# Expert layer: a ring of fifteen U blocks until the pick lists are turned, its first four blocks loaded at the end of the query projection

## The chip, the cores and the metric

The kernel runs as one launch on one core of a Trainium2 chip. The time is that of the whole launch in device microseconds (us); lower is better. Five engines work side by side: TensorE (PE, its weight loads PEld), VectorE (DVE), ScalarE (ACT), GpSimd (POOL) and SyncE (SP), which issues most of the transfers. GpSimd issues the indirect ones. Transfers between HBM and the on-chip memory are carried by 16 DMA engines.

## The reference, cut to what matters

The program is a hybrid block (`first_block`), which the change leaves alone, followed by a block of two layers. Each of those is a token mixer, a layer norm, an expert layer with 16,384 experts in which each token takes 16 for each of 8 heads, and another layer norm:

```python
def peer_ffn(h, w_query, sub_keys, expert_u, expert_v):
    q = (xt @ w_query).reshape(T, PEER_HEADS, 2, HALF_Q).astype(jnp.float32)
    scores = jnp.einsum('thpc,hpnc->thpn', q, sub_keys.astype(jnp.float32))
    top_s, top_i = lax.top_k(scores, PEER_TOPK)
    cand_s = top_s[:, :, 0, :, None] + top_s[:, :, 1, None, :]
    cand_i = top_i[:, :, 0, :, None] * N_KEYS + top_i[:, :, 1, None, :]
    ...
    best_s, best_pos = lax.top_k(cand_s, PEER_TOPK)
    idx = jnp.take_along_axis(cand_i, best_pos, axis=-1)
    gate = jax.nn.softmax(best_s, axis=-1)
    ...
    def expert_chunk(args):
        xc, ic, gc = args
        u = expert_u[ic]
        act = jax.nn.gelu(jnp.einsum('cd,ced->ce', xc, u).astype(jnp.float32), approximate=False)
        v = expert_v[ic]
        return jnp.einsum('ce,ced->cd', (gc * act).astype(v.dtype), v)
```

There are 256 tokens of width 1024, all in float32. An expert number is `i * 128 + j`, with one part from each half of the query.

## The kernel before

`second_layer` ends with two stages that matter here. `project` multiplies by `w_query_2`, fed by SyncE with slabs of the weight, while VectorE already chooses the best keys of some heads (`FirstChoice`). Then `small_experts` does the expert layer. It treats the two tiles of 128 tokens differently:

- **The dense tile** is scored against all experts. These are cut into 128 blocks of 128 experts; block n has a U block and a V block of 512 KB each. `dense(n)` on TensorE takes U block n and the turned tokens in 8 matmuls to the scores, `gelu(n)` on ScalarE writes the activation to slot `n % E`, `gate(n)` on VectorE multiplies it by the gates, and `back(n)` multiplies it by V block n in two matmuls of 512 columns.
- **The sparse tile** has for each of its 128 picks one row of 1 MB in all (u and v of each token's own expert, called a pair row), gathered by GpSimd (`load_picks`). `pick(s)` on VectorE takes one product with a running sum (L2688), ScalarE makes the share of it (`share`, L2611 and L2613), and one pick later VectorE adds the scaled v half (L2699).

All instructions stand in a fixed order on each engine, written by loops. In the order of TensorE: the scores of the keys; `LISTS_AFTER` (41) dense blocks; the turning of the pick lists (`turn_lists`, L2514), for which VectorE must have chosen the picks of the dense tile (`select(1)`, ending at L2805); 16 groups of `spread` (L2522), which turn one-hot rows into the gate matrix G, with dense blocks between them up to block E (68); `sum_gates`; then `back(0)` to `back(127)` with the other N − E blocks spread evenly over the first `DENSE_SPAN` (104) of them. VectorE slips the first 15 picks into `select(1)` and one into each of the 16 groups; the others lie beside the backs. ScalarE does the share of pick s after the gelu that `SHARES_AFTER[s]` names, and the exponentials of the gates after those in `EXP_AFTER`.

SyncE issues the U loads in block order. A U block goes to one of `RAW_U` = 4 places and waits until the block that had the place is scored (`load_u`, L2456). V blocks have 7 places; three are loaded at U blocks 5 to 7, four when G is made; from V block 10 on GpSimd gathers only those rows that some token chose (L2660). Pair rows have a ring of 4. Each ring place has a semaphore of its own.

The memory: `all_gates` (128 KB of each partition) holds G in its first half; before G exists, that half holds the query columns, the keys and what the selection works on. The upper part holds the four U places, the pair ring and the turned tokens. An arena of 68 KB holds the activation slots, the V places and, over the last four V places, the one-hot buffers.

Of the kernel before, what the change touches and what calls it, by code (L numbers as in the profile page):

```python
# [23 lines left out]
P = 128  # L24
# [170 lines left out]
def project(nc, S, name, rows, weights, slabs, cols=None, norm_scale=None, evacuate=None, scaled=None, loads=(),  # L195
            raw=None, banks=tuple(range(BANKS)), ring=2, act_from=None, beside=None, norm=None,
            ahead=None, above=0, tops_early=False, extra=None, late_loads=(), also=None, busy=(0, 0, 0, 0), loads_last=False, heads=None):
# [28 lines left out]
    with phase(nc, "slab_in0 slab_in1 slab_in2 unit_done squares mean_sq rstd_root rstd_done rows_scaled "  # L226
# [2117 lines left out]
EARLY = 68  # L2344
RAW_U, RAW_V = 4, 7
RING = 4
# [6 lines left out]
def small_experts(nc, S, layer, spare, norm):  # L2353
# [3 lines left out]
    N, E, PICKS = NKEYS, EARLY, PH * TOPK  # L2357
# [14 lines left out]
    with phase(nc, "dve_step x_turned h_full_done scores_done scores_out exp_ready exp_done rows_done lists_t lists_out "  # L2372
# [3 lines left out]
        phase(nc, "u_in0 u_in1 u_in2 u_in3 v_in0 v_in1 v_in2 v_in3 v_in4 v_in5 v_in6 row_in0 row_in1 row_in2 row_in3 "  # L2376
# [3 lines left out]
        u_in, v_in = landed[:RAW_U], landed[RAW_U:RAW_U + RAW_V]  # L2380
        row_in, some_in = landed[RAW_U + RAW_V:RAW_U + RAW_V + RING], landed[RAW_U + RAW_V + RING:]
# [40 lines left out]
        upper = S["upper"]  # L2422
        raw_u = upper([P, RAW_U, D])
# [13 lines left out]

        def slot(n):
            return act[:, n % E, :]
# [10 lines left out]
        with nc.Block() as block:  # L2450
            @block.sync
            def _(sp):
                def load_u(n):
                    if n >= RAW_U:
                        sp.wait_ge(scored, n - RAW_U + 1)
                    sp.dma_start(raw_u[:, n % RAW_U, :], ud(n)).then_inc(u_in[n % RAW_U], 16)  # L2456

                def load_v(n):
                    if n >= RAW_V:
                        sp.wait_ge(y_done, n - RAW_V + 1)  # L2460
                    sp.dma_start(raw_v[:, n % RAW_V, :], vd(n)).then_inc(v_in[n % RAW_V], 16)

                for n in range(E):
                    load_u(n)
                    if 5 <= n < 8:
                        load_v(n - 5)
                for n in range(E, E + RAW_U):
                    load_u(n)
                sp.wait_ge(g_done, SPREAD)
                for n in range(3, RAW_V):  # L2470
                    load_v(n)
                for n in range(N):
                    if n + RAW_V < WHOLE:
                        load_v(n + RAW_V)
                    for m in dense_after(n):
                        if m + RAW_U < N:
                            load_u(m + RAW_U)
                    if n == DENSE_SPAN:
                        sp.wait_ge(scored, N)
                        sp.dma_start(raw_u[:, 0, :], one_row(S, "ln2_g_2", layer)).then_inc(ln_in, 16)  # L2480
                        sp.dma_start(raw_u[:, 1, :], one_row(S, "ln2_b_2", layer)).then_inc(ln_in, 16)

            @block.tensor
            def _(pe):
# [16 lines left out]
                def dense(n):  # L2501
                    bank = (4 if n < E else 0) + n % 2
                    pe.wait_ge(u_in[n % RAW_U], 16 * (n // RAW_U + 1))
                    if n >= 2:
                        pe.wait_ge(acted, n - 1)
                    for c in range(KD):
                        last = nc.tensor.matmul(PS[:, bank, 0:P], raw_u[:, n % RAW_U, c * P:(c + 1) * P], h_full[:, c, :],  # L2507
                                                start=(c == 0), stop=(c == KD - 1), skip_group_check=True)
                    last.then_inc(scored, 1)
# [535 lines left out]
def second_layer(nc, S, layer, base, norm_of):  # L3045
    dram = S["dram"]
    if True:
# [57 lines left out]
        with ExitStack() as peer:  # L3105
# [14 lines left out]
            S["idx"] = spare([P, 2 * PH, TOPK]).bitcast(U32)  # L3120
            with phase(nc, "head_scored head_copied head_chosen") as (_, head_scored, head_copied, head_chosen):
# [73 lines left out]
```

## Time and profile before

| | us |
|---|---|
| median of 3 runs | 2655.43 |
| lowest and highest of them | 2653.43, 2655.89 |
| the profiled execution | 2652.92 |
| its span | 2651.1 |

Shares of the span: TensorE 87%, VectorE 57%, ScalarE 24%, GpSimd 23%; mean DMA rate 300 GB/s. The two expert layers reach from about 1147 to 1794 and from about 2000 to the end of the span. A busy TensorE is not one at its peak, and in rings of buffers an engine that waits for a transfer may be at the end of a chain of such waits. So the page's totals are read only to find the stages, and each stage is then read by its own windows, waits and order of time. 1.8 us of the profiled execution lie outside its span.

### The profile page before, as it was taken

The page shows a single profiled execution, that of the slowest core. Times are in us where ns is not written, and L with a number is a line of the kernel's source. Part 1 is how long each engine was busy: PE and PEld are TensorE (multiplying, and loading weights), DVE is VectorE, ACT ScalarE, POOL GpSimd, SP SyncE. Part 2 cuts the span into 40 slices and gives each one's busy share as a digit, 9 for nine tenths or more (in the row PEclk, how much of TensorE's full clock was granted, in tenths as well). Part 3 has the DMA queues.
Part 4 walks back from the last instruction along what each step waited for, and adds up shares of the span by engine and source line. Part 5 has one row for each costly group of instructions (what it writes and reads, how often), then busy time and mean ns, then how long its engine had stood idle before and what let it go on. Part 6 is the DMA issues. An engine that isn't in the chain of part 4 may idle for free. (4 is left out here: it accounts for less than half of the span.)

```text
span 2651.1 us, 42435 instructions
## 1 busy us (share of the span) xinstructions
PE 2312.0 (87%) x16666; PEld 1696.5 (64%) x16668; DVE 1514.8 (57%) x2992; ACT 627.9 (24%) x1546; POOL 599.8 (23%) x637
## 2 busy tenths in 40 slices
PE   8988988999998779987898888878998699888885
PEld 8987875555544377787875555528788597554542
DVE  4787552211100045589976566675468996666666
ACT  4543322100000036322321111114532232111111
POOL 0011200111111000001224454540000223454453
PEclk9999989999999989999899999999999999999999
DMA  7420025999999863369999999987237989999997
GB/s 224 152 73 3 3 112 213 407 418 419 419 419 420 362 220 128 105 226 385 350 398 411 408 406 412 403 338 247 76 120 268 397 341 408 407 405 403 405 402 280
DMA packets 223238, 794.92 MB, mean 300 GB/s; under 512 B 37909, under 2 KB 103957, under 8 KB 165312
## 3 DMA queue, kind: packets, MB, share of 16 engines
q1 hardware_dynamic: 148496, 443.86, 43.4%
q0 software_dynamic: 74544, 348.34, 33.2%
q8 instruction: 134, 2.20, 0.3%
q14 instruction: 64, 0.52, 0.1%
HBM read 881.07 MB, written 11.27 MB: 337 GB/s over the span
## 5 line engine op out<-in xcount | busy, mean ns | idle before, releaser
L2540 PE MATMUL psum<-v_raw,act 128*128 128x512 f32 x1024 | 500.4, 621 | 144.0 <-DMA v_raw<-expert_v_dram,all_gates 143.7
L2507 PEld LDWEIGHTS psum<-all_gates 128*128 128x128 f32 x4096 | 501.2, 198 | 115.9 <-issue 64.8
L2507 PE MATMUL psum<-all_gates 128*128 128x128 f32 x4096 | 512.0, 282 | 44.1 <-DMA all_gates<-expert_u_dram 41.0
L2652 POOL DMA_INDIRECT all_gates<-expert_pairs_dram,all_gates x256 | 260.8, 1019 | 1117.4 <-DVE all_gates L2795 500.0
L2540 PEld LDWEIGHTS psum<-v_raw,act 128*128 128x128 f32 x1024 | 182.0, 193 | 371.2 <-DMA v_raw<-expert_v_dram,all_gates 220.9
L2688 DVE CUSTOM_DVE_ANT_0 all_gates<-all_gates,psum 128x1024 f32<-128x1024 f32 x194 | 236.8, 1221 | 305.5 <-DMA all_gates<-expert_pairs_dram,all_gates 303.5
L2699 DVE SCALAR_TENSOR_TENSOR psum<-all_gates,psum 128x1024 f32<-128x1024 f32 x254 | 326.1, 1284 | 1.0 <-ACT all_gates L2613 0.7
L1754 PE MATMUL psum<-piece_raw,tile_cols 128*64 128x256 f32 x2496 | 287.9, 381 | 17.8 <-DMA piece_raw<-w_up_dram 7.7
L1754 PEld LDWEIGHTS psum<-piece_raw,tile_cols 128*64 128x64 f32 x2496 | 176.7, 137 | 129.3 <-issue 35.5
L2660 POOL DMA_INDIRECT v_raw<-expert_v_dram,all_gates x236 | 234.1, 992 | 77.8 <-issue 70.8
L2611 ACT ACTIVATE all_gates<-all_gates 128x1 f32<-128x1 f32 x256 | 51.6, 201 | 753.6 <-DVE all_gates L2688 753.6
L1834 DVE TENSOR_TENSOR hidden<-silu,psum 128x256 f32<-128x256 f32 x39 | 16.4, 421 | 276.4 <-PE psum L1754 276.4
L454 PE MATMUL psum<-in_cols,in_top 128*128 128x256 f32 x864 | 160.2, 287 | 8.9 <-DVE in_low L362 3.9
L1789 PE MATMUL psum<-piece_raw,hidden_cols 128*64 128x512 f32 x624 | 143.2, 595 | 10.5 <-DMA piece_raw<-w_down_dram 10.1
L454 PEld LDWEIGHTS psum<-in_cols,in_top 128*128 128x128 f32 x864 | 135.3, 193 | 11.9 <-issue 7.3
L346 DVE TENSOR_TENSOR in_low<-in_raw,in_top 128x2048 fp32r<-128x2048 f32 x38 | 87.0, 2290 | 68.1 <-ACT in_top L297 68.1
L454 PE MATMUL psum<-in_cols,in_low 128*128 128x256 f32 x432 | 122.8, 284 | 0.0
L2592 ACT ACTIVATE act<-psum 128x128 f32<-128x128 f32 x256 | 67.9, 268 | 217.2 <-PE psum L2507 216.8
L1812 ACT ACTIVATE silu<-psum 128x256 f32<-128x256 f32 x39 | 15.0, 385 | 415.9 <-PE psum L1754 415.9
L1840 DVE COPY tile_result<-psum 128x512 f32<-128x512 f32 x39 | 27.0, 691 | 130.4 <-PE psum L1789 130.4
L1789 PEld LDWEIGHTS psum<-piece_raw,hidden_cols 128*64 128x64 f32 x624 | 43.8, 137 | 88.2 <-issue 70.0
L2832 DVE TENSOR_TENSOR act<-act,all_gates 128x128 f32<-128x128 f32 x256 | 90.4, 374 | 6.5 <-ACT all_gates L2596 6.5
(541 smaller groups left out, 3392.4 us busy)
## 6 DMA issues: line engine op xcount, KB each, us to landing
all_gates<-expert_u_dram SPq DMA_DIRECT2D x256, 512.0 KB, 7.7
piece_raw<-w_gate_dram SPq DMA_DIRECT2D x78, 1024.0 KB, 19.5
piece_raw<-w_up_dram SPq DMA_DIRECT2D x78, 1024.0 KB, 21.6
piece_raw<-w_down_dram SPq DMA_DIRECT2D x78, 1024.0 KB, 22.7
in_raw<-w_in_dram SPq DMA_DIRECT2D x48, 1024.0 KB, 5.2
query_raw<-w_query_dram SPq DMA_DIRECT2D x16, 1024.0 KB, 5.5
v_raw<-expert_v_dram SPq DMA_DIRECT2D x20, 512.0 KB, 7.3
w_o<-w_o_dram SPq DMA_DIRECT2D x16, 512.0 KB, 11.1
```

Source lines behind the costliest of these rows:

```text
L346: nc.vector.tensor_tensor(r32(lows[place[s]]), raw[:, s % RING, :, :], tops[place[s]], ALU.subtract).then_inc(slab_low, 1)
L454: last = nc.tensor.matmul(PS[:, banks[n % len(banks)], half * T:(half + 1) * T], r32(lhs), r32(rhs), start=(k == 0 and i == 0), stop=(k == ...
L1754: last = nc.tensor.matmul(PS[side(g), bank, 0:WIDE], window[:, t % 2, k, :], raw[:, n % RAW, at:at + WIDE], start=(k == 0), stop=(k == KD ...
L1789: last = nc.tensor.matmul(PS[side(g), OUT[t % 2], :], hid_cols[:, c, q - 4, :], raw[:, n % RAW, at:at + HALF], start=(q == 4 and c == 0), ...
L2507: last = nc.tensor.matmul(PS[:, bank, 0:P], raw_u[:, n % RAW_U, c * P:(c + 1) * P], h_full[:, c, :], start=(c == 0), stop=(c == KD - 1), s ...
L2540: last = nc.tensor.matmul(PS[:, 4 + m, :], slot(n), raw_v[:, n % RAW_V, m * BANK:(m + 1) * BANK], start=(n == 0), stop=(n == N - 1), skip_ ...
L2592: nc.scalar.activation(slot(n), PS[:, bank, 0:P], ACT.Gelu).then_inc(acted, 1)
L2652: nc.gpsimd.indirect_dma_start(out=ring[:, r, :, :].rearrange("p h d -> p (h d)"), out_offset=None, in_=S["pair_rows"], in_offset=bass.Ind ...
L2660: nc.gpsimd.indirect_dma_start(out=raw_v[:, n % RAW_V, :], out_offset=None, in_=S["v_rows"], in_offset=bass.IndirectOffsetOnAxis(ap=load_r ...
L2688: nc.vector.tensor_tensor_reduce(row, row, own, 1.0, 0.0, ALU.mult, ALU.add, own_sum[:, s:s + 1]).then_inc(dotted, 1)
L2699: stt(both, row, own_share[:, c:c + 1], both, ALU.mult, ALU.add).then_inc(picked_done, 1)
L2832: tt(slot(n), slot(n), G[:, :, n], ALU.mult).then_inc(gated, 1)
```

## The change

Four things are done together:

- The U ring has 15 places until block 45: the four old ones, four over the one-hot buffers of the arena, and seven over the query columns and keys at the start of `all_gates`. From block 45 on it is the ring of 4 again. The first load into the seven waits until all key scores are made. Eleven more semaphores go with it.
- The loads of blocks 0 to 3 stand at the end of SyncE's part of the query projection, through a new argument `behind`. Their four semaphores are made in a phase of their own around the projection and the expert layer.
- E goes from 68 to 80: `EARLY` = 72 slots in the arena, 8 more in `all_gates` behind G. The blocks spread beside the backs are 48 in place of 60.
- `LISTS_AFTER` goes from 41 to 52, `EXP_AFTER` from (8, 38) to (8, 49), and the shares move to later gelus.

```diff
+                if behind is not None:
+                    behind(sp)
                 if loads:
                     sp.wait_ge(loaded, 16 * (len(loads) + len(late_loads)))
...
-EARLY = 68
+EARLY = 72
+MORE = 8
 RAW_U, RAW_V = 4, 7
+OVER_HOTS, OVER_QUERY = 4, 7
+WIDE_U = RAW_U + OVER_HOTS + OVER_QUERY
+WIDE_UNTIL = 3 * WIDE_U
...
-    N, E, PICKS = NKEYS, EARLY, PH * TOPK
+    N, E, PICKS = NKEYS, EARLY + MORE, PH * TOPK
...
-    EXP_AFTER = (8, 38)
-    LISTS_AFTER = 41
+    EXP_AFTER = (8, 49)
+    LISTS_AFTER = 52
...
-    SHARES_AFTER = (19, 20, 21, 23, 24, 26, 28, 29, 30, 32, 34, 35, 36, 38, 39)
+    SHARES_AFTER = (21, 22, 24, 26, 28, 31, 34, 36, 39, 41, 44, 46, 47, 49, 50)
...
+        def u_place(n):
+            return n % WIDE_U if n < WIDE_UNTIL else (n - WIDE_UNTIL) % RAW_U
+
+        def u_before(n):
+            return max((m for m in range(n) if u_place(m) == u_place(n)), default=None)
...
         def slot(n):
-            return act[:, n % E, :]
+            return act[:, n % E, :] if n % E < EARLY else more_act[:, n % E - EARLY, :]
...
                 def load_u(n):
-                    if n >= RAW_U:
-                        sp.wait_ge(scored, n - RAW_U + 1)
-                    sp.dma_start(raw_u[:, n % RAW_U, :], ud(n)).then_inc(u_in[n % RAW_U], 16)
+                    if u_before(n) is not None:
+                        sp.wait_ge(scored, u_before(n) + 1)
+                    if n == RAW_U + OVER_HOTS:
+                        sp.wait_ge(scores_done, len(BATCHES[0]) + len(BATCHES[1]))
+                    sp.dma_start(u_buffer(n), ud(n)).then_inc(u_in[u_place(n)], 16)
...
                 for n in range(E):
-                    load_u(n)
+                    if n >= RAW_U:
+                        load_u(n)
                     if 5 <= n < 8:
                         load_v(n - 5)
...
+            def first_blocks(sp):
+                for n in range(RAW_U):
+                    sp.dma_start(S["raw_u"][:, n, :], S["u_src"](n)).then_inc(first_u_in[n], 16)
```

The queue of SyncE in the first layer, from the last slabs of the query weight into the expert layer. Before (L268 loads slabs, L2456 U blocks, L2461 V blocks):

```order
L268 DMA query_raw_11086<-w_query_dram 128x8x256 x5
L252 UNCONDITIONAL_BRANCH
L2451 UNCONDITIONAL_BRANCH
L2456 DMA all_gates<-expert_u_dram 128x1024 x6
L2461 DMA v_raw_12104<-expert_v_dram 128x1024
...
L2456 DMA all_gates<-expert_u_dram 128x1024 x64
L2461 DMA v_raw_12104<-expert_v_dram 128x1024 x6
```

Now (L3159 is `first_blocks`, L2485 the other U loads, L2490 V blocks):

```order
L268 DMA query_raw_11086<-w_query_dram 128x8x256 x5
L3159 DMA all_gates<-expert_u_dram 128x1024 x4
L252 UNCONDITIONAL_BRANCH
L2478 UNCONDITIONAL_BRANCH
L2485 DMA u_over_hots_12111<-expert_u_dram 128x1024 x2
L2490 DMA v_raw_12109<-expert_v_dram 128x1024
...
L2485 DMA all_gates<-expert_u_dram 128x1024 x11
L2485 DMA u_over_hots_12111<-expert_u_dram 128x1024 x4
L2485 DMA all_gates<-expert_u_dram 128x1024 x11
L2485 DMA u_over_hots_12111<-expert_u_dram 128x1024 x4
L2485 DMA all_gates<-expert_u_dram 128x1024 x46
L2490 DMA v_raw_12109<-expert_v_dram 128x1024 x7
```

Four U loads moved from behind the branch between the two stages to a place ahead of it, and the U loads ahead of the V blocks that wait for G are 84 in place of 72.

TensorE in the first layer, from the first dense block to the second group of the gate matrix; a dense block is 8 matmuls. Before (L2507 dense, L2514 the lists, L2522 a group):

```order
L2507 MATMUL psum<-all_gates 128x128 x328
L2514 MATMUL psum<-constants_51,all_gates 128x128 x4
L2522 MATMUL psum<-hot_j_12108,hot_i_12106 128x128 x8
L2507 MATMUL psum<-all_gates 128x128 x8
L2522 MATMUL psum<-hot_j_12108,hot_i_12106 128x128 x8
```

Now (L2537 dense, L2544 the lists, L2552 a group):

```order
L2537 MATMUL psum<-all_gates 128x128 x32
L2537 MATMUL psum<-all_gates,u_over_hots_12111 128x128 x32
L2537 MATMUL psum<-all_gates 128x128 x88
L2537 MATMUL psum<-all_gates,u_over_hots_12111 128x128 x32
L2537 MATMUL psum<-all_gates 128x128 x88
L2537 MATMUL psum<-all_gates,u_over_hots_12111 128x128 x32
L2537 MATMUL psum<-all_gates 128x128 x112
L2544 MATMUL psum<-constants_51,all_gates 128x128 x4
L2552 MATMUL psum<-hot_j_12115,hot_i_12113 128x128 x8
L2537 MATMUL psum<-all_gates 128x128 x8
```

Ahead of the lists there are 416 dense matmuls (52 blocks) in place of 328 (41 blocks), and the places of their U blocks go round the wide ring.

## Rows read from the trace of the kernel before

**Rows 1.** page, part 2: the span in 40 slices of 66.3 us each
```profile
DMA  7420025999999863369999999987237989999997
GB/s 224 152 73 3 3 112 213 407 418 419 419 419 420 362 220 128 105 226 385 350 398 411 408 406 412 403 338 247 76 120 268 397 341 408 407 405 403 405 402 280
```

**Rows 2.** stages of layer one: window, busy us (x instructions), clock, DMA share, GB/s
```profile
1148.50:1265.70 117.20, 89.82 (x704) 85.43 (x703) 106.84 (x405) 29.26 (x86) 18.50 (x18) 0.93 0.95 361
1271.50:1351.00 79.50, 78.90 (x678) 78.38 (x679) 76.94 (x91) 30.47 (x74) 18.40 (x16) 0.97 0.93 353
1352.00:1722.00 370.00, 317.34 (x1415) 196.25 (x1415) 229.10 (x354) 51.25 (x224) 177.04 (x179) 0.97 1.02 409
1722.00:1782.00 60.00, 40.78 (x83) 15.01 (x82) 43.25 (x64) 9.44 (x35) 33.05 (x34) 0.97 0.97 379
```

**Rows 3.** the same view in windows of ten us, both layers
```profile
1130.00:1140.00 10.00, 10.00 (x87) 10.00 (x85) 8.73 (x30) 2.67 (x3) 0.00 (x0) 1.00 0.01 2
1150.00:1160.00 10.00, 10.00 (x92) 10.00 (x91) 9.83 (x57) 5.50 (x11) 0.00 (x0) 1.00 0.75 266
1160.00:1170.00 10.00, 8.33 (x72) 7.95 (x72) 9.83 (x63) 1.11 (x4) 0.00 (x0) 1.00 1.00 375
...
1270.00:1280.00 10.00, 8.46 (x54) 8.46 (x55) 10.00 (x12) 2.59 (x7) 1.97 (x2) 0.67 0.40 137
2000.00:2010.00 10.00, 9.25 (x83) 9.28 (x84) 8.76 (x54) 5.91 (x10) 0.00 (x0) 1.00 0.63 222
```

**Rows 4.** DMA, 1193 to 1262: queues, then issues with us to landing
```profile
DMA packets 5424, 26.70 MB, mean 387 GB/s; under 512 B 607, under 2 KB 607, under 8 KB 3729
...
q0 software_dynamic: 1902, 13.84, 50.2%
q1 hardware_dynamic: 3516, 12.79, 48.0%
...
all_gates<-expert_u_dram SPq DMA_DIRECT2D x24, 512.0 KB, 9.0
all_gates<-expert_pairs_dram,all_gates POOLq DMA_INDIRECT x13, 9.4
```

**Rows 5.** SyncE queue in order of time: start, us, line, what
```profile
1107.48 18.08 SPq L268 DMA_DIRECT2D query_raw<-w_query_dram  x4
1147.77 2.00 SPq L2456 DMA_DIRECT2D all_gates<-expert_u_dram  x4
```

**Rows 6.** TensorE in order of time, first layer
```profile
1153.67 10.88 PE L2507 MATMUL psum<-all_gates 128*128 128x128 f32 x96
...
1265.75 1.12 PE L2514 MATMUL psum<-constants,all_gates 128*128 128x128 f32 x4 [6.99 <-DVE all_gates L2805]
1271.54 3.78 PE L2522 MATMUL psum<-hot_j,hot_i 128*128 128x128 f32 x16 [4.67 <-DVE hot_j L2825]
...
1352.41 7.14 PE L2530 MATMUL psum<-all_gates,ident_half 128*128 128x512 bf16 x31
```

**Rows 7.** VectorE in order of time, first layer
```profile
1192.47 1.22 DVE L2688 CUSTOM_DVE_ANT_0 all_gates<-all_gates,x 128x1024 f32<-128x1024 f32 x1
...
1202.44 1.29 DVE L2696 TENSOR_SCALAR psum<-all_gates 128x1024 f32<-128x1024 f32 x1 [6.05 <-ACT all_gates L2613]
...
1261.79 1.22 DVE L2688 CUSTOM_DVE_ANT_0 all_gates<-all_gates,x 128x1024 f32<-128x1024 f32 x1 [2.52 <-DMA all_gates<-expert_pairs_dram,all_gates]
...
1265.40 0.29 DVE L2805 TENSOR_TENSOR all_gates<-all_gates 128x128 f32<-128x128 f32 x1
```

**Rows 8.** waits, 1352 to 1782: total us, times, longest
```profile
DVE all_gates L2688 <- DMA all_gates<-expert_pairs_dram,all_gates: 152.8, 93, 3.8
...
PEld psum L2540 <- DMA v_raw<-expert_v_dram,all_gates: 109.2, 63, 4.5
```

**Rows 9.** end of the program in order of time
```profile
2641.94 2.48 DVE L2280 SCALAR_TENSOR_TENSOR x<-x,ln_stats,all_gates 128x1024 f32<-128x1024 f32 x2
2646.25 0.40 SPq L2885 DMA_DIRECT2D out_dram<-x  x1
```

More of the change, by code:

```diff
@@ L196, in project @@
             raw=None, banks=tuple(range(BANKS)), ring=2, act_from=None, beside=None, norm=None,
-            ahead=None, above=0, tops_early=False, extra=None, late_loads=(), also=None, busy=(0, 0, 0, 0), loads_last=False, heads=None):
+            ahead=None, above=0, tops_early=False, extra=None, late_loads=(), also=None, busy=(0, 0, 0, 0), loads_last=False, heads=None, behind=None):
     PS, C = S["psum"], S["const"]
@@ L2350, with small_experts @@
 UPPER_FLOATS = RAW_U * D + RING * 2 * D + KD * P + 7 * PH * TOPK
-def small_experts(nc, S, layer, spare, norm):
+def small_experts(nc, S, layer, spare, norm, first_u_in):
     PS, C = S["psum"], S["const"]
     HP = 2 * PH
-    N, E, PICKS = NKEYS, EARLY, PH * TOPK
+    N, E, PICKS = NKEYS, EARLY + MORE, PH * TOPK
     DENSE, SPARSE = 0, 1
@@ L2379, in small_experts @@
             memory3, ln_in, scored, acted, gated, y_done, picked_done, quarter_done, root_ready, root_done):
-        u_in, v_in = landed[:RAW_U], landed[RAW_U:RAW_U + RAW_V]
-        row_in, some_in = landed[RAW_U + RAW_V:RAW_U + RAW_V + RING], landed[RAW_U + RAW_V + RING:]
+        over = OVER_HOTS + OVER_QUERY
+        u_in, v_in = list(first_u_in) + list(landed[:over]), landed[over:over + RAW_V]
+        row_in, some_in = landed[over + RAW_V:over + RAW_V + 8], landed[over + RAW_V + 8:]
         KB = 1024
@@ L2421, in small_experts @@
         number = spare([P, P])
-        upper = S["upper"]
-        raw_u = upper([P, RAW_U, D])
+        upper, raw_u = S["upper"], S["raw_u"]
         ring = upper([P, RING, 2, D])
@@ L2436, in batch_number, with u_turn, u_buffer @@
             return turn * len(BATCHES[0]) + BATCHES[turn].index(n) + 1
+        u_over_query = S["all_gates"][:, 0:OVER_QUERY * D // NKEYS, :].rearrange("p (b r) j -> p b (r j)", b=OVER_QUERY)
+        def u_place(n):
+            return n % WIDE_U if n < WIDE_UNTIL else (n - WIDE_UNTIL) % RAW_U
+        def u_turn(n):
+            return sum(u_place(m) == u_place(n) for m in range(n + 1))
+        def u_before(n):
+            return max((m for m in range(n) if u_place(m) == u_place(n)), default=None)
+        def u_buffer(n):
+            place = u_place(n)
+            if place < RAW_U:
+                return raw_u[:, place, :]
+            if place < RAW_U + OVER_HOTS:
+                return u_over_hots[:, place - RAW_U, :]
+            return u_over_query[:, place - RAW_U - OVER_HOTS, :]
         def slot(n):
-            return act[:, n % E, :]
+            return act[:, n % E, :] if n % E < EARLY else more_act[:, n % E - EARLY, :]
         def picks_after(n):
@@ L2506, in dense @@
                     for c in range(KD):
[L2507 removed]
+                        last = nc.tensor.matmul(PS[:, bank, 0:P], u_buffer(n)[:, c * P:(c + 1) * P], h_full[:, c, :],
                                                 start=(c == 0), stop=(c == KD - 1), skip_group_check=True)
@@ L3120, in second_layer @@
             S["idx"] = spare([P, 2 * PH, TOPK]).bitcast(U32)
+            u, v = dram["expert_u_2"], dram["expert_v_2"]
+            S["u_src"] = lambda j: u[bass.ds(layer * NKEYS + j, 1), :, :, :].rearrange("j p k i -> (j p) k i")
+            S["v_src"] = lambda j: v[bass.ds(layer * NKEYS + j, 1), :, :].rearrange("j i d -> (j i) d")
+            S["raw_u"] = S["upper"]([P, RAW_U, D])
+            first_u_in = peer.enter_context(phase(nc, "u_in0 u_in1 u_in2 u_in3"))[1:]
+            def first_blocks(sp):
+                for n in range(RAW_U):
+                    sp.dma_start(S["raw_u"][:, n, :], S["u_src"](n)).then_inc(first_u_in[n], 16)
             with phase(nc, "head_scored head_copied head_chosen") as (_, head_scored, head_copied, head_chosen):
@@ L3124, in second_layer @@
                         raw=ahead["raw"], loads=[(S["keys"], one("sub_keys_2", "p e n"))], norm=between, ahead=ahead,
-                        above=3 * 16 * KB, banks=(0, 1, 2, 3, 4, 5),
+                        above=3 * 16 * KB, banks=(0, 1, 2, 3, 4, 5), behind=first_blocks,
                         heads=FirstChoice(nc, S, head_scored, head_copied, head_chosen))
-            u, v = dram["expert_u_2"], dram["expert_v_2"]
-            S["u_src"] = lambda j: u[bass.ds(layer * NKEYS + j, 1), :, :, :].rearrange("j p k i -> (j p) k i")
-            S["v_src"] = lambda j: v[bass.ds(layer * NKEYS + j, 1), :, :].rearrange("j i d -> (j i) d")
             S["pair_rows"] = dram["expert_pairs_2"][:, :]
             S["v_rows"] = v.rearrange("j i d -> (j i) d")
-            small_experts(nc, S, layer, spare, norm_of("ln2_b_2", layer, None) if layer + 1 < LAYERS else None)
+            small_experts(nc, S, layer, spare, norm_of("ln2_b_2", layer, None) if layer + 1 < LAYERS else None, first_u_in)
 def layout(inputs):
```

8 lines of the change are left out of this document (5 added, 3 removed).

## The prediction

> **What bounds the kernel now.** I read the page's 40 slices first [rows 1]. In slices 18 to 26 and 31 to 39, counted from 0, DMA stands near 9 tenths and mostly about 400 GB/s: the expert layers are streams of transfers. The slices also show holes where those layers begin. So I cut the first expert layer into its stages [rows 2]. Stage A reaches from the first U load (1148.5) to the turned lists (1265.7): DMA share 0.95, but only 361 GB/s. Stage B (1271.5 to 1351), the 16 groups: 353 GB/s, while TensorE is busy 78.90 of 79.50 us and VectorE 76.94. Stage C (1352 to 1722), backs with U blocks beside them: share 1.02, 409 GB/s. Stage D (1722 to 1782), backs without U blocks: 379 GB/s.
>
> Stage C is bound by DMA. TensorE is idle 53 of 370 us there and VectorE 141, GpSimd 193, and over C and D the large waits all end with a transfer: VectorE 152.8 us for pair rows, TensorE's weight loads 109.2 us for V rows [rows 8]. No engine's work fills the stage, and the two streams that wait share the same 16 engines with U. So its length follows its bytes: what is loaded before G is made need not be loaded in C.
>
> The ten-us windows show where DMA has room [rows 3]. From 1130 to 1140 it moves 2 GB/s: the last query slab is issued by 1125.6 and the first U load only at 1147.77 [rows 5]. In 1150 to 1160 the share is 0.75 and 266 GB/s. With only U moving and the share at 1.00 (1160 to 1170) it still gives 375 GB/s, and TensorE, waiting for blocks, is busy 8.33 of 10. The second layer starts in the same way (2000 to 2010: 0.63, 222 GB/s).
>
> What ends stage A is VectorE: the lists were turned at 1265.75 after a wait of 6.99 for L2805, which starts at 1265.40 [rows 6, 7]. VectorE has two pauses on its way: 6.05 us before 1202.44, when ScalarE's first share stands behind the gelu of block 19, which TensorE gets late, and 2.52 us for a pair row before 1261.79.
>
> **The change part by part, per layer.** A U block is 512 KB, 0.524 MB.
>
> 1. Stage C loses blocks. E goes from 68 to 80, so 12 fewer blocks, 12 × 0.524 = 6.29 MB. At C's own 409 GB/s that is **15.4 us less**. TensorE also loses 12 × 1.8 = 22 us of work there (1.8 us a block: six blocks in 10.88 [rows 6]), so it gets no closer to being the bound. Bounds of the term: 15.4 if the rate stays, 16.6 at D's 379, 0 if the stage did not follow its bytes.
>
> 2. Stage A must load more before the lists. Before: 361 GB/s × 117.2 us = 42.3 MB; of it 41 + 4 U blocks (23.6 MB) and 3 V blocks (1.6), which leaves 17.1 MB of pair rows. Now 52 blocks must be there, but four came early: 48 × 0.524 = 25.2, with V and the same pair rows 43.9 MB. The only question is the rate. At 409 that takes 107.3 us, at 387 (the mean of 1193 to 1262 [rows 4]) 113.4, at the 375 of U alone 117.1. With 1.8 us for the last block the lists could be turned at 1257.6, 1263.7 or 1267.4. VectorE sets the other limit: without its 6.05 us pause L2805 starts at 1259.4. That pause should go: share 0 now stands behind block 21, and 22 blocks are scored by 1153.7 + 22 × 1.8 = 1193.3 if they have landed; by then DMA at 375 has moved 16.8 MB, less V and about 3 MB of pair rows, 23 blocks and the early four. I take the middle rate: lists at about 1263.7, **2 us earlier**, with bounds of 6 earlier and 2 later from these rates.
>
> The early four transfers are issued behind the last slab and take 2.1 / 0.409 = 5 us in a stretch where DMA moves 2 GB/s; nothing is queued behind them but the stage's end, and TensorE is still full with the projection in 1130 to 1140. I charge nothing for them; were they in the way, it would be by at most those 5 us. The load of block 8 now waits for the last key score; behind it on SyncE stand only further U loads, and the four blocks and three V blocks ahead of it (3.7 MB, 9 us at 409) cover from 1148.5 to 1157, past the first dense block at 1153.67, which follows those scores.
>
> 3. Stage B gets one block more (28 instead of 27), and TensorE is full there [rows 2]: **1.8 us more**; none if VectorE's groups, 76.94 us of the 79.5, hide it. I take the full price, since TensorE has the longer busy time.
>
> 4. One more phase is left at the layer's end. At the program's end VectorE finishes at 2644.42 and the store is issued at 2646.25 [rows 9], 1.8 us for three such exits and the end of the block. So at most **0.6 us more** for the fourth with its semaphores; at least 0.
>
> Later gelus move the exponentials of the gates too: gelu 49 comes two blocks before the lists, as gelu 38 did. ScalarE is busy 29 of 117 us in A and takes it. Activation slots in another buffer change no instruction's shape.
>
> Sum per layer: −15.4 − 2 + 1.8 + 0.6 = −15.0. Two layers: −30. The sum is made against the profiled execution, 2652.9, and gives 2622.9. The median of the runs stands 2.5 above that execution, so the forecast is **2625.4**, rounded to 2625. The best ends (−15.4 − 6 + 0 + 0.3) give −21 a layer and about 2613.
>
> **A rule weighed.** In 1193 to 1262 both queues have work nearly always, and they share the time evenly, 50.2% for the pair rows and 48.0% for U, with some 3 U blocks (24 × 9.0 / 69) and 2 pair rows (13 × 9.4 / 69) under way [rows 4]. In the Trainium skill, page "DMA: Bandwidth & Descriptors", section "Queues, rings and completion order", each DMA engine goes round-robin between the queue rows that have work. By that rule fifteen U places take no larger share than four, and the pair rows keep their pace; the trace agrees with an even split but has no stretch with a deep U queue. If the share instead followed what each queue has outstanding, the third rival below would come about.
>
> **The rivals.**
>
> *The lists come later, but the gain in C stays.* VectorE needs a pair row about every 69 / 13 = 5.3 us in A, at 200 GB/s. A U queue that never runs dry can slow a few of them, and TensorE's position holds VectorE back through the shares: a late block 41 delays share 9, and so on. If the lists are 5 to 12 us late instead of 2 early, a layer gains 8 to 1 us: 2640 to 2653, its middle 2646. For it: the pause of 2.52 at 1261.79 shows that pair rows are sometimes short. Against: the bytes of A fit at the rate that the same stretch has today.
>
> *Stage C does not shorten.* If V and pair rings were bound by their own round trips (7 and 4 places, transfers of some 9 to 10 us), U blocks would have used spare room. Then only −2 + 1.8 + 0.6 remains, nothing: 2656. Against it: share 1.02 and 409 GB/s over 370 us.
>
> *Slower: the deep U queue starves the pair rows.* Ten blocks outstanding (5.2 MB) against two or three pair rows: U then runs at TensorE's pace, 0.524 / 1.8 = 291 GB/s, and leaves 118 for pair rows, one in 9 us instead of 5.3. From 1193 until TensorE has its 52 blocks (1247) that makes 6 picks and not 10; the four missing ones cost 5.3 us each with their part of the selection, 21 us, before the lists can be turned. A layer then changes by −15.4 + 21 + 2.4 = +8: 2671. It decides once the lists come more than 13 us later. Against it: the even split above.
>
> *More than forecast.* The deep queue brings A to C's 409 GB/s, the lists are turned at about 1260 and stage B hides its block: 2613 to 2616.
>
> **How the numbers follow.** Forecast, 2617 to 2635: 0.56. More: 0.13. Lists late, 2635 to 2652: 0.18. C not shorter: 0.07. Slower by starvation: 0.06. The range 2612 to 2648 leaves out the slow cases and the upper part of the late one, about 2 in 10. A measurement of this kernel can tell 0.2%, 5.3 us, from no change. Faster by more than that: 0.87 (forecast, more, nearly all of lists late); within it 0.07; slower 0.06.
>
> **What would show it.** Right: 1130 to 1140 carries about 2 MB; stage A runs at 380 GB/s or more; no pause of VectorE before its first L2699-type sum; the lists within a few us of 1264; from the first back to the last U block about 15 us shorter at the same 409 GB/s; the same once more in the second layer. Wrong: pair waits of VectorE in A of 10 us or more, lists after 1270, or a stage C with the share well under 1.0.

## The result and the profile after

| | us |
|---|---|
| before, median of 4 runs (lowest, highest) | 2655.66 (2653.43, 2659.43) |
| changed, median of 4 runs (lowest, highest) | 2620.23 (2616.91, 2624.52) |
| ratio of changed to before, 95% interval | 0.9866, 0.9847 to 0.9885 |
| the profiled execution of the changed kernel, its span | 2619.32, 2617.6 |

The change saves 35 us, 1.3%. The forecast was 2625, 30 us less; 2620 was measured. In this document stage A is now measured from the first dense block to the turning of the lists, B from there to `sum_gates`, C from there to the last dense block, D to the last back. All four come from the order of time of TensorE:

| us | A | B | C | D | all |
|---|---|---|---|---|---|
| before, layer 1 | 112.1 | 86.7 | 368.2 | 65.8 | 632.8 |
| before, layer 2 | 109.5 | 88.4 | 364.5 | 68.4 | 630.8 |
| changed, layer 1 | 108.0 | 87.4 | 351.6 | 68.1 | 615.1 |
| changed, layer 2 | 108.2 | 88.2 | 347.5 | 70.9 | 614.8 |

The two layers sum to 33.7 us less, and the spans differ by 33.5 (2651.1, 2617.6), so the rest of the program gives nothing on balance.

The page of the changed kernel, part 2 (40 slices of 65.4 us), answers to [rows 1]. Slice 18, in stage A in both kernels, carries 414 GB/s, where it was 385:

```profile
DMA  7420024999999964269999999996338999999997
GB/s 223 147 84 3 3 114 168 392 419 419 419 419 419 419 220 150 89 254 414 352 402 410 405 413 406 396 377 212 116 113 317 408 352 403 407 406 399 411 400 269
```

The stages of the first layer in the changed kernel, columns as in [rows 2]:

```profile
1148.50:1263.40 114.90, 105.74 (x884) 104.05 (x885) 107.18 (x406) 31.58 (x96) 18.81 (x18) 0.96 0.99 396
1268.70:1350.00 81.30, 81.27 (x699) 81.08 (x700) 77.43 (x93) 30.14 (x75) 18.43 (x16) 0.96 0.95 366
1351.00:1702.00 351.00, 290.38 (x1213) 169.74 (x1212) 225.78 (x349) 48.93 (x210) 175.31 (x177) 0.98 1.01 406
1702.00:1766.00 64.00, 43.77 (x90) 16.24 (x90) 46.10 (x68) 10.02 (x37) 34.60 (x35) 0.95 0.97 382
```

Stage A moves 396 GB/s and not 361. C keeps its rate (406; 409 before) and is shorter. B is full of TensorE's work as before.

In windows of ten us, against [rows 3]:

```profile
1130.00:1140.00 10.00, 10.00 (x86) 10.00 (x85) 8.08 (x21) 4.04 (x5) 0.00 (x0) 1.00 0.69 265
1140.00:1150.00 10.00, 8.12 (x69) 7.94 (x68) 5.79 (x33) 0.98 (x2) 0.00 (x0) 1.00 0.00 0
1150.00:1160.00 10.00, 10.00 (x92) 10.00 (x91) 9.69 (x56) 6.18 (x11) 0.00 (x0) 1.00 0.95 350
1160.00:1170.00 10.00, 10.00 (x92) 10.00 (x91) 9.86 (x62) 1.47 (x6) 0.00 (x0) 1.00 1.03 412
1270.00:1280.00 10.00, 10.00 (x71) 10.00 (x71) 10.00 (x11) 3.29 (x8) 2.40 (x2) 0.76 0.60 205
1990.00:2000.00 10.00, 10.00 (x92) 10.00 (x91) 9.86 (x59) 2.20 (x7) 0.00 (x0) 1.00 1.02 409
```

1130 to 1140 has the early blocks (2.65 MB in all instead of 0.02). From 1150 on DMA is nearly full at once, and 1160 to 1170 has 412 GB/s, where 375 stood, with TensorE busy 10.00 instead of 8.33. A hole of ten us is left at 1140 to 1150, between the landing of the early blocks and the start of the stage, and the one behind the lists (1270 to 1280) stays.

SyncE's queue in order of time answers to [rows 5]; the four early loads follow the last slab directly:

```profile
1109.21 18.08 SPq L268 DMA_DIRECT2D query_raw<-w_query_dram  x4
1127.34 2.32 SPq L3159 DMA_DIRECT2D all_gates<-expert_u_dram  x4
...
1155.62 7.47 SPq L2485 DMA_DIRECT2D all_gates<-expert_u_dram  x11
```

TensorE in order of time, for [rows 6]. In brackets: us idle and what ended them. The trace has two records for each matmul of a dense block, so 16 records are one block.

```profile
1155.42 7.31 PE L2537 MATMUL psum<-all_gates 128*128 128x128 f32 x64
...
1169.72 20.15 PE L2537 MATMUL psum<-all_gates 128*128 128x128 f32 x176
...
1241.29 13.92 PE L2537 MATMUL psum<-all_gates 128*128 128x128 f32 x96 [2.68 <-DMA all_gates<-expert_u_dram]
1257.76 5.81 PE L2537 MATMUL psum<-all_gates 128*128 128x128 f32 x32 [2.55 <-DMA all_gates<-expert_u_dram]
1263.41 0.60 PE L2544 MATMUL psum<-constants,all_gates 128*128 128x128 f32 x4
1268.68 3.78 PE L2552 MATMUL psum<-hot_j,hot_i 128*128 128x128 f32 x16 [4.67 <-DVE hot_j L2855]
...
1350.86 7.14 PE L2560 MATMUL psum<-all_gates,ident_half 128*128 128x512 bf16 x31
```

176 records, 11 blocks, follow each other in 20.15 us, 1.8 us a block, without a wait. The few waits for U blocks stand at the end of the stage, from block 41 on. That is before the ring has 4 places again (block 45), so the small ring alone doesn't make them. The lists are turned at 1263.41 with no wait for VectorE at all. VectorE itself, for [rows 7]:

```profile
1198.07 1.28 DVE L2726 TENSOR_SCALAR psum<-all_gates 128x1024 f32<-128x1024 f32 x1
...
1257.68 1.23 DVE L2718 CUSTOM_DVE_ANT_0 all_gates<-all_gates,x 128x1024 f32<-128x1024 f32 x1 [1.32 <-DMA all_gates<-expert_pairs_dram,all_gates]
...
1261.31 0.29 DVE L2835 TENSOR_TENSOR all_gates<-all_gates 128x128 f32<-128x128 f32 x1
1264.75 0.69 DVE L2846 TENSOR_TENSOR eighths<-constants,lists 128x512 bf16<-128x512 f32 x1 [3.15 <-ACT lists L2654]
```

The pause of 6.05 us is gone (L2726 now follows at once), and the last row of the selection starts at 1261.31. VectorE was ready 1.8 us ahead of the lists: the end of A now hangs on TensorE, which waits for its last blocks.

DMA in 1193 to 1240, against [rows 4], with a deep U queue:

```profile
DMA packets 3864, 19.48 MB, mean 414 GB/s; under 512 B 434, under 2 KB 434, under 8 KB 2545
...
q0 software_dynamic: 1487, 10.76, 55.6%
q1 hardware_dynamic: 2371, 8.65, 45.8%
...
all_gates<-expert_u_dram SPq DMA_DIRECT2D x11, 512.0 KB, 28.8
u_over_hots<-expert_u_dram SPq DMA_DIRECT2D x3, 512.0 KB, 22.3
all_gates<-expert_pairs_dram,all_gates POOLq DMA_INDIRECT x9, 9.5
```

U blocks take 22.3 to 28.8 us from issue to landing instead of 9.0, since they stand in a long queue; pair rows take 9.5 us, as before (9.4). By these rows some 8 U blocks are under way ((11 × 28.8 + 3 × 22.3) / 47) where there were 3, and still 2 pair rows (9 × 9.5 / 47).

The deep ring brings its U blocks earlier, in the stretch ahead of this one. In 1150 to 1193 the queue of U and V moves 15.16 MB and not 11.10. In 1193 to 1240 it moves 8.65 MB against 8.68 before, and what grows there are the pair rows, 10.76 MB against 9.02, since VectorE no longer pauses. 8.65 MB are some 16 blocks, while TensorE scores about 23 in these 47 us (an estimate, from its rows above): it lives on the stock, which is used up about block 41.

### The profile page after: what moved, and what is told of

It is laid out like the page before. It is cut to its first block and busy times, and to the rows that moved or that the text cites. A ratio compares the mean times of both kernels' runs of the same rounds, so it can differ in the third digit from the quotient of the medians.

```text
span 2617.6 us, 42437 instructions
## 1 busy us (share of the span) xinstructions
PE 2303.2 (88%) x16666; PEld 1688.0 (64%) x16668; DVE 1514.4 (58%) x2992; ACT 630.1 (24%) x1546; POOL 599.7 (23%) x637
## 3 DMA queue, kind: packets, MB, share of 16 engines
q0 software_dynamic: 74544, 348.34, 33.5%
## 5 line engine op out<-in xcount | busy, mean ns | idle before, releaser
L2570 PE MATMUL psum<-v_raw,act 128*128 128x512 f32 x960 | 469.3, 624 | 147.8 <-DMA v_raw<-expert_v_dram,all_gates 147.7
L2537 PEld LDWEIGHTS psum<-all_gates 128*128 128x128 f32 x3712 | 449.2, 197 | 73.5 <-issue 52.0
L2537 PE MATMUL psum<-all_gates 128*128 128x128 f32 x3712 | 455.8, 281 | 19.2 <-DMA all_gates<-expert_u_dram 17.6
L2570 PEld LDWEIGHTS psum<-v_raw,act 128*128 128x128 f32 x960 | 172.6, 194 | 376.9 <-DMA v_raw<-expert_v_dram,all_gates 229.4
L1756 PEld LDWEIGHTS psum<-piece_raw,tile_cols 128*64 128x64 f32 x2496 | 177.8, 138 | 131.0 <-issue 38.0
L2690 POOL DMA_INDIRECT v_raw<-expert_v_dram,all_gates x236 | 234.7, 995 | 76.7 <-issue 70.9
L1791 PEld LDWEIGHTS psum<-piece_raw,hidden_cols 128*64 128x64 f32 x624 | 43.8, 137 | 87.1 <-issue 68.9
L456 PE MATMUL psum<-query_cols,query_top 128*128 128x256 f32 x512 | 93.6, 285 | 0.1
## 6 DMA issues: line engine op xcount, KB each, us to landing
piece_raw<-w_up_dram SPq DMA_DIRECT2D x78, 1024.0 KB, 20.4
```

The source lines that it names most:

```text
L456: last = nc.tensor.matmul(PS[:, banks[n % len(banks)], half * T:(half + 1) * T], r32(lhs), r32(rhs), start=(k == 0 and i == 0), stop=(k == ...
L1756: last = nc.tensor.matmul(PS[side(g), bank, 0:WIDE], window[:, t % 2, k, :], raw[:, n % RAW, at:at + WIDE], start=(k == 0), stop=(k == KD ...
L1791: last = nc.tensor.matmul(PS[side(g), OUT[t % 2], :], hid_cols[:, c, q - 4, :], raw[:, n % RAW, at:at + HALF], start=(q == 4 and c == 0), ...
L2537: last = nc.tensor.matmul(PS[:, bank, 0:P], u_buffer(n)[:, c * P:(c + 1) * P], h_full[:, c, :], start=(c == 0), stop=(c == KD - 1), skip_g ...
L2570: last = nc.tensor.matmul(PS[:, 4 + m, :], slot(n), raw_v[:, n % RAW_V, m * BANK:(m + 1) * BANK], start=(n == 0), stop=(n == N - 1), skip_ ...
L2690: nc.gpsimd.indirect_dma_start(out=raw_v[:, n % RAW_V, :], out_offset=None, in_=S["v_rows"], in_offset=bass.IndirectOffsetOnAxis(ap=load_r ...
```

## The experiments

Times are medians, ratios with their 95% intervals against the kernel before on the same chip. The stages are those of one profiled execution of each kernel, layer 1 / layer 2:

| kernel | us | ratio | A | B | C | D |
|---|---|---|---|---|---|---|
| e1, ring and early loads, old order | 2640.98 | 0.9930 (0.9906 to 0.9954) | 103.5 / 103.9 | 87.4 / 89.0 | 371.2 / 364.2 | 66.8 / 68.9 |
| e2, order alone | 2668.97 | 1.0050 (1.0032 to 1.0068) | 131.0 / 128.3 | 87.4 / 88.0 | 350.3 / 347.0 | 69.5 / 68.6 |
| e3, no early loads | 2632.33 | 0.9913 (0.9881 to 0.9944) | 112.6 / 113.1 | 87.4 / 87.6 | 351.5 / 348.4 | 69.6 / 68.3 |
| e4, early loads, ring of 4 | 2666.14 | 1.0035 (1.0018 to 1.0051) | 126.9 / 131.7 | 88.1 / 87.8 | 352.2 / 347.8 | 68.8 / 69.6 |
| e10, as e4, old shares | 2669.70 | 1.0060 (1.0037 to 1.0083) | 129.9 / 132.4 | 88.6 / 87.7 | 351.2 / 347.2 | 68.8 / 68.8 |
| e11, ring of 8 | 2632.86 | 0.9918 (0.9899 to 0.9938) | 115.9 / 113.9 | 87.5 / 87.1 | 351.7 / 345.8 | 69.1 / 70.5 |
| e6, half the U bytes in C | 2573.28 | 0.9693 (0.9657 to 0.9729) | 105.0 / 108.9 | 87.2 / 88.9 | 327.0 / 327.1 | 69.8 / 67.2 |
| e5, two blocks in the wait | 2614.60 | 0.9842 (0.9809 to 0.9876) | 106.9 / 109.5 | 89.0 / 86.0 | 349.5 / 348.0 | 68.5 / 68.9 |
| e7, lists after 50, two in the wait | 2620.27 | 0.9874 (0.9838 to 0.9910) | 105.0 / 105.8 | 89.0 / 88.1 | 351.9 / 351.0 | 68.0 / 68.3 |
| e8, six early blocks | 2618.91 | 0.9857 (0.9816 to 0.9897) | 104.9 / 104.2 | 89.9 / 87.3 | 352.2 / 347.7 | 69.8 / 70.9 |
| e9, e5 and e8 together | 2611.02 | 0.9844 (0.9825 to 0.9862) | 105.8 / 105.8 | 87.9 / 88.1 | 350.1 / 345.9 | 68.3 / 68.9 |
| e12, the change again | 2619.41 | 0.9866 (0.9845 to 0.9887) | 107.6 / 108.9 | 88.0 / 87.7 | 351.2 / 348.9 | 69.1 / 68.6 |

How far can one execution's stages be trusted? Up to the lists the changed kernel, e5, e6 and e12 run the same code, and their A is 105.0 to 108.0 us in the first layer and 108.2 to 109.5 in the second. So a difference of 3 us in the first layer's A says nothing by itself.

### The parts of the change

My theory was that the gain is bytes moved out of stage C, and that the ring and the early loads pay for them in A. The rivals gave it to one part alone.

**e1**, against the changed kernel:

```diff
-EARLY = 72
+EARLY = 60
...
-    EXP_AFTER = (8, 49)
-    LISTS_AFTER = 52
+    EXP_AFTER = (8, 38)
+    LISTS_AFTER = 41
...
-    SHARES_AFTER = (21, 22, 24, 26, 28, 31, 34, 36, 39, 41, 44, 46, 47, 49, 50)
+    SHARES_AFTER = (19, 20, 21, 23, 24, 26, 28, 29, 30, 32, 34, 35, 36, 38, 39)
```

> The wide ring and the early loads stay; E is 68 again, the lists are turned after 41 blocks, shares and exponentials stand where they stood before. Theory 'bytes moved out of stage C': no block leaves C, so only VectorE's pause of 6 us in stage A goes; A 5 to 7 us shorter a layer, B and C as before: 2641 to 2646. Rival 'the deep ring itself brings the gain': about 2620.

2641, as the theory says. A is 6 to 9 us shorter, C is not. It also shows the floor of A: 103.5 to 103.9 us, which VectorE needs for the selection with its picks. In the first layer it waits for pair rows for only 0.2 us in all there, and TensorE waits 5.0 us for it before the lists.

**e2**: the changed kernel with `u_place(n) = n % RAW_U` for every n and without `first_blocks`.

> Order and E of the change (80, lists after 52), but a ring of 4 throughout and the first four blocks loaded when the stage starts. Theory: C 14 to 15 us shorter, but A has to load 11 blocks (5.8 MB) more through the shallow ring, 12 to 16 us longer; sum near nothing: 2648 to 2660. Rival 'the order alone brings the gain, transfers keep up anyway': about 2620 to 2625.

2669, slower than the kernel before. C gives its 17.5 to 18 us, but A costs 19 more; I had expected 12 to 16.

**e3**: only `first_blocks` is taken away; blocks 0 to 3 are loaded at the start of the stage.

> As the change, but blocks 0 to 3 are loaded when the stage starts. Theory: 2.1 MB more in the saturated stage A, 4 to 5 us a layer: about 2629. Rival 'the deep ring catches up, early loads bring nothing': 2620.

The four early blocks are worth 4.6 and 4.9 us of A, close to the 5 of their transfers. (The median, 2632, is above the profiled execution's 2624, to which these stages belong.)

**e4**: the changed kernel with the ring of 4:

```diff
-            return n % WIDE_U if n < WIDE_UNTIL else (n - WIDE_UNTIL) % RAW_U
+            return n % RAW_U
```

> As the change, but a ring of 4 throughout; the early loads stay. Theory: stage A loses what the deep ring gives (shares of 0.75 to 0.9 in its first 40 us), 8 to 11 us longer than in the change, C as in the change: 2636 to 2645. Rival 'the early loads are the part that counts': 2620 to 2625.

Both theories missed: 2666. Without the deep ring the early loads bring nothing that can be seen (A 126.9 and 131.7 against e2's 131.0 and 128.3). One reason shows in e4's windows, columns as above. The four early blocks hold all four places until the first of them is scored, so the load of block 4 is issued at 1157.64, and DMA moves 3 GB/s in a stretch in which e2 moves 250:

```profile
1150.00:1158.50 8.50, 8.50 (x78) 8.50 (x78) 8.04 (x48) 5.91 (x10) 0.00 (x0) 1.00 0.01 3
```

The trace also has a wait that I had left out of my count, VectorE for ScalarE's share (us in total, times, longest):

```profile
PE psum L2537 <- DMA all_gates<-expert_u_dram: 23.2, 17, 5.2
DVE psum L2729 <- ACT all_gates L2643: 12.9, 5, 3.3
DVE psum L2726 <- ACT all_gates L2643: 10.2, 1, 10.2
```

VectorE stands still 23 us because shares follow gelus whose blocks are late. Is that the cause or only a companion of the slow loads? **e10** puts the shares and exponentials back to the gelus of before:

```diff
-    EXP_AFTER = (8, 49)
+    EXP_AFTER = (8, 38)
...
-    SHARES_AFTER = (21, 22, 24, 26, 28, 31, 34, 36, 39, 41, 44, 46, 47, 49, 50)
+    SHARES_AFTER = (19, 20, 21, 23, 24, 26, 28, 29, 30, 32, 34, 35, 36, 38, 39)
```

> The ring of 4 with early loads, E 80 and lists after 52, but shares and exponentials at the gelus of before (19 to 39, and 38). It asks why stage A takes 127 to 132 us with the small ring. Theory 'load rate': 45.5 MB at 345 to 361 GB/s are 126 to 132 us whatever VectorE does: A unchanged, 2664. Rival 'late shares hold VectorE back (it waits 10 to 13 us for the first)': A 115 to 118, about 2640.

A stays at 129.9 and 132.4. The wait only moves: VectorE is done early and then waits 21.9 us for the lists, which TensorE turns late.

```profile
PE psum L2537 <- DMA all_gates<-expert_u_dram: 24.7, 20, 2.8
...
DVE eighths L2846 <- ACT lists L2654: 21.9, 1, 21.9
```

So it is the rate at which the ring can load that sets A. Over A itself, from the first dense block to the lists, the first layer moves 362 GB/s before, 347 in e4 and 360 in e10 with 4 places, 384 in e11 with 8, and 406 in the changed kernel. The cause of the rate shows in a stretch in which U blocks are nearly all that moves, 1155 to 1180. The kernel before, then the changed one (queue, packets, MB, share of time; then issues with us to landing):

```profile
DMA packets 2047, 7.47 MB, mean 299 GB/s; under 512 B 227, under 2 KB 227, under 8 KB 2045
...
q1 hardware_dynamic: 2045, 7.45, 85.5%
...
all_gates<-expert_u_dram SPq DMA_DIRECT2D x12, 512.0 KB, 4.6
```

```profile
DMA packets 2774, 10.14 MB, mean 406 GB/s; under 512 B 306, under 2 KB 306, under 8 KB 2771
...
q1 hardware_dynamic: 2771, 10.10, 101.6%
...
all_gates<-expert_u_dram SPq DMA_DIRECT2D x16, 512.0 KB, 10.7
```

And SyncE's own waits in the kernel before, 1150 to 1180:

```profile
SPq L2456 <- PE psum L2507: 23.5, 12, 5.9
```

With 4 places, of which TensorE holds one or more, a block lands in 4.6 us but SyncE waits 23.5 of 30 us for the block in the next place to be scored, and the DMA engines have nothing to do for 14% of the 25 us above. With 15 places their share is 1.02, and they move 406 GB/s and not 299.

**e11** asks how deep is enough; the ring has 8 places until block 40, then 4.

```diff
-            return n % WIDE_U if n < WIDE_UNTIL else (n - WIDE_UNTIL) % RAW_U
+            return n % EIGHT if n < 5 * EIGHT else n % RAW_U
```

> The change with a ring of 8 (the four old places and four over the one-hot buffers) until block 40, then 4. How deep must the ring be? In the change a U block lands 10.7 us after its issue with all DMA engines full, and 8 blocks are 10.3 us of transfers at 409 GB/s. Theory 'enough in flight to cover the time from issue to landing': 8 places give A of 108 to 111, 2620 to 2626. Rival 'all 15 are needed, since pair rows drain the ring for 50 us': A 115 to 120, 2635 to 2645.

A is 115.9 and 113.9, between the two ranges that I gave: 8 places win 11 and 18 us of A over the 4 of e4, which has the same shares, and 15 places another 8 and 6. TensorE still waits 16.7 us for blocks, and VectorE 7.8 for shares behind them:

```profile
PE psum L2538 <- DMA all_gates<-expert_u_dram: 10.6, 9, 2.7
...
DVE psum L2730 <- ACT all_gates L2644: 7.8, 5, 2.9
...
PE psum L2538 <- DMA u_over_hots<-expert_u_dram: 6.1, 7, 1.7
```

### Does stage C follow its bytes?

In every kernel with 48 blocks beside the backs and whole U loads C is 13 to 19 us shorter than before, but those kernels also spare TensorE 12 blocks of work. **e6** separates the two by leaving out half the bytes of 44 blocks, and with them part of the result:

```diff
-                    sp.dma_start(u_buffer(n), ud(n)).then_inc(u_in[u_place(n)], 16)
+                    to, src = u_buffer(n), ud(n).rearrange("p k i -> p (k i)") if len(ud(n).shape) == 3 else ud(n)
+                    if n >= E + RAW_U:
+                        to, src = to[:, 0:D // 2], src[:, 0:D // 2]
+                    sp.dma_start(to, src).then_inc(u_in[u_place(n)], 16)
```

> The changed kernel, but of the U blocks from 84 on (44 of the 48 beside the backs) only the first half is loaded, so 44 x 0.262 = 11.5 MB a layer less at the same work of TensorE; their second half is left out of the computation as old data. Theory 'stage C follows its bytes': 11.5 / 0.409 = 28 us a layer less in C, some 2564. Rival 'C followed TensorE's work, 12 blocks x 1.8 us': C unchanged, 2620. Rival 'rings bound by round trips': nearly unchanged too.

With TensorE's work unchanged C goes from 351.6 and 347.5 to 327.0 and 327.1, 24.6 and 20.4 us less. Columns as in the windows above:

```profile
1350.00:1676.00 326.00, 283.18 (x1212) 166.23 (x1210) 225.99 (x349) 49.21 (x210) 175.59 (x177) 1.00 1.02 402
2163.00:2489.00 326.00, 285.43 (x1212) 168.33 (x1211) 225.64 (x347) 48.89 (x210) 175.47 (x177) 0.99 1.01 396
```

The number of transfers and TensorE's work are as they were. So C follows its bytes and neither of the two, nor round trips. It falls short of the 28 us of the theory; the rate is 402 and 396 GB/s in place of 406 and 405, which is 3 to 7 us of the 326. Why the rate is lower is open.

### What is left in A and B

**e5** (E 82, blocks 52 and 53 between the lists and the first group, on TensorE and ScalarE):

```diff
                 turn_lists()
-                at_block = LISTS_AFTER
+                for n in range(LISTS_AFTER, LISTS_AFTER + IN_GAP):
+                    dense(n)
+                at_block = LISTS_AFTER + IN_GAP
...
```

> Between the turning of the lists and the first group TensorE waits 4.67 us for one-hot rows. Two dense blocks are put there and E goes to 82. Theory: TensorE's wait holds them (3.6 us), stage B keeps its length (87.4 to 88.2 from lists to the sums), C loses 2 blocks, 2.8 us a layer: about 2615. Rival 'their U blocks are not there in time, B grows by what C loses': 2620. If the first group is held up, B grows by up to 2 us: 2619.

2614.6 was forecast as 2615, but its interval does not part it from the changed kernel, and it did not go as I wrote. In the first layer the two blocks had to be waited for (1.00 and 0.74 us), and B is 1.6 us longer than in the changed kernel (and 2.2 shorter in the second layer):

```profile
1267.19 0.60 PE L2545 MATMUL psum<-constants,all_gates 128*128 128x128 f32 x4
1268.79 2.05 PE L2538 MATMUL psum<-all_gates 128*128 128x128 f32 x16 [1.00 <-DMA all_gates<-expert_u_dram]
1271.58 2.05 PE L2538 MATMUL psum<-all_gates 128*128 128x128 f32 x16 [0.74 <-DMA all_gates<-expert_u_dram]
```

**e7** takes E back to 80, turns the lists after 50 blocks and leaves two in the wait; the shares and exponentials stand one or two gelus earlier, too.

> The changed kernel with E 80, but the lists are turned after 50 blocks and blocks 50 and 51 stand in TensorE's wait behind them; shares and exponentials one or two gelus earlier. Theory: TensorE's late blocks, not VectorE, end stage A in the changed kernel (lists at 1263.4, VectorE done at 1261.6), so A is 2 to 4 us shorter, B and C the same: 2612 to 2616. Rival 'VectorE ends A': A unchanged, 2620.

A is 3.0 and 2.4 us shorter, as the theory says, though only the second layer's 105.8 lies below what the same code gives (108.2 to 109.5). TensorE waits for VectorE again (6.16 us before the lists). But B is 0.8 us longer on the mean of the layers and C 1.9, and the time is 2620 where 2612 to 2616 was expected: not to be told from the change.

```profile
1260.83 1.12 PE L2545 MATMUL psum<-constants,all_gates 128*128 128x128 f32 x4 [6.16 <-DVE all_gates L2840]
```

**e8** loads blocks 4 and 5 early too, into the buffer that the selection writes later; VectorE waits for block 5 before it writes there:

```diff
+                    if turn == 0:
+                        dve.wait_ge(scored, RAW_U + OVER_PICKED)
...
+                for n in range(OVER_PICKED):
+                    sp.dma_start(S["u_over_picked"][:, n, :], S["u_src"](RAW_U + n)).then_inc(first_u_in[RAW_U + n], 16)
```

> The changed kernel with blocks 4 and 5 loaded early too, into the buffer that the selection writes later (L2801), whose first write waits for block 5. Theory: stage A is bound by its bytes, 2 x 0.524 MB less of them is 2.6 us a layer: about 2615, A near 105.5. Rival 'A is bound by VectorE or by the ring of 4 from block 45 on': A unchanged, 2620.

A is 104.9 and 104.2, 3 to 4 us less and within 1.4 us of VectorE's floor; again the second layer alone is clear of the spread. The time, 2619 against the 2615 expected, does not show it.

**e9** joins e5 and e8, and **e12** is the changed kernel beside it.

> The two edits together that each looked a little better than the change: six early blocks, and two dense blocks in TensorE's wait behind the lists with E 82. Theory: A near 105 (VectorE's own floor is the 103.7 of the run with the old order), B 87 to 89, C 2 to 3 us shorter: 5 us a layer less than the changed kernel, about 2610. Rival 'A ends with VectorE and B grows by what C loses': 2617 to 2620.

> The changed kernel once more, unchanged, beside the others on the same chip: 2620.

2611.0 (2610.3 to 2617.3, 5 runs) against 2619.4 (2613.1 to 2625.7, 6 runs): about 8 us by the medians and 6 by the ratios, and the stages of the profiled executions sum to 9.2 us less (612.1 + 608.6 against 615.8 + 614.1). The two intervals against before overlap (0.9825 to 0.9862, 0.9845 to 0.9887), so it is likely and not proved that e9 beats the change. A is 105.8 twice, C 1.1 and 3.0 shorter. TensorE waits for VectorE before the lists, and no longer behind them:

```profile
1262.80 1.11 PE L2553 MATMUL psum<-constants,all_gates 128*128 128x128 f32 x4 [5.92 <-DVE all_gates L2850]
1263.71 5.31 PE L2546 MATMUL psum<-all_gates 128*128 128x128 f32 x32
1268.86 1.95 PE L2561 MATMUL psum<-hot_j,hot_i 128*128 128x128 f32 x16
```

## Why the prediction was right

- **Stage C loses 12 blocks, −15.4 a layer.** C became 16.6 and 17.0 shorter, but D 2.3 and 2.5 longer, together −14.3 and −14.5. The mechanism is shown by e6. That D grows was not in the sum: it has the same 24 backs. It is seen in every kernel with fewer blocks in C for the first layer (68.0 to 69.8 against 65.8 before and 66.8 in e1), and less surely for the second (67.2 to 70.9 against 68.4 and 68.9). Pair and V rows left over when C ends sooner would explain it; what is left over was not measured.
- **Stage A, −2.** It was −4.1 in the first layer and −1.3 in the second. The same code gave 105.0 to 109.5 in other executions, so the −2 is right in direction and rough in size. The middle rate, 387 GB/s, was a little low, the stage ran at 396; my count of bytes was a little low too (43.9 MB; 396 × 114.9 is 45.5). Of what was missing, 0.9 MB are U blocks loaded ahead of the 52nd and 0.6 pair rows (27.70 MB of U and V in all, and 17.66 of pair rows). The two errors work against each other, and the stage began 1.7 us later in this execution: that the lists, forecast at 1263.7, came at 1263.41 is partly luck. VectorE's pause went, as forecast, and VectorE's floor of 103.5 (e1) lies below what the loads allow.
- **The early loads cost nothing** and are worth 4.6 to 4.9 us (e3), as their 5 us of transfers say. From the last slabs' first issue to the first dense block it is 46.2 us before (1107.48 to 1153.67) and 46.2 after (1109.21 to 1155.42).
- **Stage B, +1.8.** It was +0.7 and −0.2: the dear end of the two was taken. In the first layer the 16 groups themselves take 82.2 us instead of 80.9, and the way from the lists to them 0.5 less; in the second they take 82.6 both times.
- **The fourth phase exit, +0.6.** At the end of the program the way from VectorE's last result to the store went from 1.83 [rows 9] to 2.27 us, 0.44 more, and it is 2.27 to 2.30 in every experiment. The sum charged 0.6 in each layer, the runs show it at the end only, and they do not part the exit from its additional semaphores:

```profile
2608.00 2.48 DVE L2282 SCALAR_TENSOR_TENSOR x<-x,ln_stats,all_gates 128x1024 f32<-128x1024 f32 x2
2612.75 0.40 SPq L2915 DMA_DIRECT2D out_dram<-x  x1
```

- **The even split.** U and pair rows share the time 45.8% to 55.6% with some 8 U blocks under way instead of 3 (48.0% to 50.2% before), and pair rows land as fast as before. The rival of starvation is refuted by the trace, and the rule of the Trainium skill that I weighed, page "DMA: Bandwidth & Descriptors", section "Queues, rings and completion order", agrees with this. Only the split is seen here, not the turn-taking itself.
  The waits of VectorE for pair rows in C and D fell, too (138.6; 152.8 before [rows 8]):

```profile
DVE all_gates L2718 <- DMA all_gates<-expert_pairs_dram,all_gates: 138.6, 93, 4.2
```

- **The sum.** Over both layers C and D gave −28.8 where −30.8 was forecast, A −5.4 where it was −4, B +0.5 where it was +3.6. The cost in D that was missed takes back a part of what B was charged too much, so the forecast is as near as it is partly by luck.
- **What I missed** is how much the depth carries. I wrote "the only question is the rate" and put 375 GB/s as the pace of U alone. That row was the best ten us of a ring of 4; the 25 us around it moved 299. With the order and a ring of 4 the kernel is slower than before (e2, e4, e10): the change is right only as a whole.

## What to carry to other kernels

If a stage is bound by transfers and an earlier one has room for them, count bytes by stage: what is moved forward is saved at the late stage's rate, and costs in the early one only what its holes do not hold. Here a ring of 4 blocks of 512 KB, each place refilled only when it had been used, did not keep the DMA engines full (299 GB/s against 406 with 15). Before work is moved into a stage whose ring is shallow, see whether the DMA share of its stream has gaps, and deepen the ring if so: here the early stage lost 19 us where the late one gained 18 (e2). Memory that is dead for a while at the start of a stage was enough for it. Loads moved ahead of a stage need places of their own too: in e4 they filled the ring, and the stage began with an idle DMA.

## What was not expected of the hardware

- A stream of 512 KB blocks through 4 places moved 299 GB/s at a share of 0.86, the same stream through 15 places 406 GB/s at 1.02 (1155 to 1180).
- A U queue in which a block takes 28.8 us from issue to landing did not slow the other queue's 1 MB gathers (9.5 against 9.4 us).
- The same code took 105.0 to 108.0 us in one stage, from one execution to another. A difference of 2 to 4 us is at the edge of what one trace can show, and is lost in medians of 4 runs, which spread by 7 to 14 us here (e5, e7, e8).
